# A first query projection without the token factor, a value projection woven into the recurrence's inverse, level masks on VectorE, and later output loads

## The chip, the core and the metric

The kernel runs on one core of one Trainium2 chip. The metric is the device time of one execution in microseconds (us); less is better. The engines are TensorE (PE; PEld are its weight loads), VectorE (DVE), ScalarE (ACT), GpSimd (POOL) and SyncE (SP), which issues most DMAs.

## The reference, cut to what matters

Three blocks run one after the other on 256 tokens of 1024 features, all in float32: a hybrid layer with three attentions and 16 experts, two attention layers, and two layers of feed-forward, gating (SGU) and an RWKV7 mixer. The change touches the first lines of the first block and the RWKV7 mixer of the third.

```python
def rmsnorm(x, g):
    y = x * lax.rsqrt(jnp.mean(x * x, axis=-1, keepdims=True) + EPS)
    return y * g
...
h = rmsnorm(x, attn_norm_g)
proj = h @ w_in                      # its first 1024 columns are da_q
...
# rwkv7_mixer; 16 heads of 64
xx = shifted(x) - x
r, k, v = (x + xx * mu[i]) @ w_rkv[i]
w = -softplus(-(w0 + tanh(xw @ w1) @ w2)) - 0.5
a = sigmoid(a0 + (xa @ a1) @ a2)
g = sigmoid(xg @ g1) @ g2
kk = k * k_k / norm(k * k_k);  k = k * (1 + (a - 1) * k_a)
# per token, with decay = exp(-exp(w)), a_t = -kk, b_t = kk * a:
state = state * decay + (state @ a_t) b_t^T + v k^T;  y = state @ r
y = groupnorm(y) * gn_g + gn_b
out = ((y + sum(r * k * r_k) * v) * g) @ w_o
```

## The kernel before

**Products in three terms.** Weights and activations of a dense product are split into a rounded high half and the rest ("hi" and "lo", type float32r). `t_three` (lines 582 to 584) makes each product from three matmuls: hi x hi, hi x lo, lo x hi. ACT makes the weights' high half (`a_hi`, line 544), DVE the low half (`v_lo`, line 555), each in two halves of a load of 1 MB, 128x1024 elements each. A load sits in a staging slot (four slots: units 32, 34, 36, 38 of on-chip memory, names `U_(u, n)`); its halves go to a "pair" of buffers. A slot is loaded again once both halves are made, a pair is written again once TensorE has used it (`pair_free`). `plan` writes the order of all loads; `sync` issues them in that order on SP, so that a load that waits holds back those behind it. `a_upto`, `a_ahead` and `v_upto`, `v_ahead` convert loads in order up to a number.

**The order of the work** on each engine is written by hand, with semaphores between engines; each engine runs its own list in order. PSUM has eight banks, handed out in turn by `Ring` (`FB`: 0 to 3, `KB`: 0 to 7); who takes a bank waits for the one who read it last.

**The start.** `t_mix`, `a_mix`, `v_mix` begin with the norm of x: ACT squares (line 886), TensorE sums them over features with a matrix of ones (line 877), ACT takes the root (904), DVE the reciprocal (`v_rstd`, 909: RSTD, one factor for each token), then eight times x times gain times RSTD (916, DVE), the high half (899, ACT) and the low half (922, DVE). TensorE runs eight filler matmuls (`t_idle`, 627) and then the four chunks of "daq", 48 matmuls of 256 columns each, whose results ACT evacuates (835). "dak" follows.

**The RWKV7 mixer.** `t_rwkv`, `a_rwkv`, `v_rwkv`, `g_rwkv`. TensorE makes k, the small products of w and a, and r, then z3 and z4 (line 2698, the gate's first product), the value projection "rwkv.v" (`t_proj_tm`, four chunks, each in two halves of 24 matmuls), and the gate's second product (2709, 2710). Meanwhile ACT makes the sigmoids of z3, z4 and then the three exponentials of the summed decay ("grow", 2955; "decay_before", 2959; "decay", 2962), and DVE the decayed b, a, k and r (3128, 3133, 3138, 3145) and the values without their mean (3152 to 3158).

The recurrence is done in chunks of 64 tokens: for each chunk and head a triangular 64x64 system is inverted. `t_cells` (2631) makes the 64 cells of one kind, 64x64 matmuls in float32, which the trace shows as 128 rows. First N, its transpose NT, the a rows by token (2726) and A2T. The inverse T doubles in five levels: X = (NT times the level's mask) T; T's transpose G by `to_g` (2740), and T = T + G X. ACT copies X and G (2984, 2993), DVE adds (3193). The masks of level 1 are DVE's (3180), those of levels 2 to 5 GpSimd's (3286). In each level TensorE has other work as well, `fill`: b and k by token (955), RBT, RKT with the bonus rows (2673), Z with the bonus (2763); DVE masks or copies these (3168, 3199). Behind the inverse come the changes of the chunks (2790), W1, W2, MT and QT (2807), the outputs (2823, at whose end stands the mark "chunks"), the passing of the state (2845, 2836), the group norm and the output projection "rwkv.o", whose four loads are all issued early.

## Time and profile before

| | |
|---|---|
| time, median of 3 runs | 2775.74 us (2774.43 to 2778.12) |
| the profiled execution: time, span | 2778.7 us, 2776.7 us |
| TensorE busy | 2339.0 us, 84% |
| VectorE, ScalarE, GpSimd busy | 1227.0, 931.3, 61.2 us |
| DMA | 695.46 MB, mean 250 GB/s |
| start to the first three-term matmul | 17.97 us |
| RWKV7 mixer and its surroundings | 2315 to 2580 us |
| from the first cells (N) to the first matmul behind the inverse | 2430.16 to 2509.16 us |

Times in the trace are from the start of the span; the run's time is 2.0 us longer than the span. In a timeline a line gives start, duration, engine and line of the kernel, operation, output and inputs with shapes, the number of instructions merged (x), and in brackets the idle time of that engine before it and what ended it; "issue" there means that nothing the profile shows was waited for. The PEclk of a stretch is the granted clock of TensorE, 1.00 being 2.4 GHz.

### The profile page before, as it was taken

To read this page: it belongs to the slowest core of one execution; us is meant where nothing else is said; L and a number is where in the kernel's file an instruction comes from. 1 tells how busy PE (TensorE), PEld (TensorE's weight loads), DVE (VectorE), ACT (ScalarE), POOL (GpSimd) and SP (SyncE) were. 2 spreads that over 40 slices of the span, in tenths; PEclk is the share of its full clock that TensorE was granted. 3 is DMA by queue.
4 is the path that set the end of the run, shared out by engine and by line. 5 is a ranking of instruction groups with operands and counts; after the bars stand their busy time and mean duration, and the time that the engine had idled before them with its cause. 6 is when DMAs were issued, how large, how long until landed. Compare 5 with 4: busy or idle time off the path is not lost.

```text
span 2776.7 us, 37696 instructions
## 1 busy us (share of the span) xinstructions
PE 2339.0 (84%) x16482; PEld 1668.4 (60%) x16482; DVE 1227.0 (44%) x1751; ACT 931.3 (34%) x1524; POOL 61.2 (2%) x36
## 2 busy tenths in 40 slices
PE   8999998656565565656889999999999999977998
PEld 8897785111111121111479888798887888866787
DVE  5667562000010000000387765576656548744654
ACT  5556541000000000000355654444454444632442
POOL 0000010000000000000000000000000000041000
PEclk9999999877878888887899999999999999999999
DMA  7543459999999999999734365575545553412552
GB/s 237 167 159 114 144 206 405 428 428 428 428 428 428 428 428 427 428 427 428 285 104 140 122 212 182 175 249 182 197 168 202 191 197 108 155 34 78 192 187 91
DMA packets 248645, 695.46 MB, mean 250 GB/s; under 512 B 11648, under 2 KB 191104, under 8 KB 222112
## 3 DMA queue, kind: packets, MB, share of 16 engines
q1 hardware_dynamic: 246176, 679.16, 64.3%
q0 software_dynamic: 2016, 13.67, 1.3%
q8 instruction: 130, 2.13, 0.3%
q14 instruction: 35, 0.29, 0.0%
q10 hardware_dynamic: 288, 0.22, 0.0%
HBM read 691.96 MB, written 1.05 MB: 250 GB/s over the span
## 4 chain that ended last, share of the span: by engine, by line
PE 58%; DMA 29%; DVE 8%; ACT 3%; issue 1%; SPq 1%; POOL 0%; ACTq 0%; DVEq 0%
PE ps L582 16%; PE ps L584 15%; PE ps L583 15%; DMA af<-in_w_exp_up 13%; DMA af<-in_w_exp_gate 9%; DMA af<-in_w_exp_down 6%; PE ps L1661 2%; DVE ar L555 1%; PE ps L2631 1%; SPq L513 1%; PE ps L877 1%; PE ps L1691 1%; ACT af L1057 1%; PE ps L2226 1%; DVE af L1096 1%
## 5 line engine op out<-in xcount | busy, mean ns | idle before, releaser
L582 PE MATMUL ps<-ar 128*128 128x512 f32 (+2 forms) x2648 | 925.1, 349 | 17.6 <-DVE ar L3276 2.9
L584 PE MATMUL ps<-ar 128*128 128x512 f32 (+2 forms) x2648 | 907.2, 343 | 0.0
L583 PE MATMUL ps<-ar 128*128 128x512 f32 (+2 forms) x2648 | 907.1, 343 | 0.0
L555 DVE TENSOR_TENSOR ar<-af,ar 128x1024 fp32r<-128x1024 f32 x516 | 604.2, 1221 | 288.3 <-ACT ar L544 288.2
L544 ACT ACTIVATE ar<-af 128x1024 fp32r<-128x1024 f32 x516 | 510.4, 1047 | 158.8 <-PE ps L584 142.5
L582 PEld LDWEIGHTS ps<-ar 128*128 128x128 f32 x2648 | 502.2, 190 | 93.3 <-issue 12.0
L584 PEld LDWEIGHTS ps<-ar 128*128 128x128 f32 x2648 | 502.2, 190 | 59.1
L583 PEld LDWEIGHTS ps<-ar 128*128 128x128 f32 x2648 | 502.9, 190 | 56.1 <-issue 0.5
L1661 PE MATMUL ps<-af 128*32 128x512 f32 x2048 | 329.6, 777 | 226.0 <-DMA af<-in_w_exp_up 120.0
L1661 PEld LDWEIGHTS ps<-af 128*32 128x32 f32 x2048 | 64.1, 127 | 476.1 <-DMA af<-in_w_exp_up 193.9
L1691 PE MATMUL ps<-af 128*32 128x512 f32 x1024 | 164.6, 769 | 99.9 <-DMA af<-in_w_exp_down 87.5
L1830 DVE TENSOR_TENSOR af<-af,ps 128x512 f32<-128x512 f32 x16 | 11.0, 688 | 538.0 <-ACT af L1737 538.0
L1737 ACT ACTIVATE af<-ps 128x512 f32<-128x512 f32 x16 | 9.6, 597 | 592.1 <-PE ps L1661 592.1
L1548 DVE TENSOR_TENSOR af<-ps,af 128x512 f32<-128x512 f32 x76 | 48.6, 685 | 296.1 <-PE ps L1703 273.5
L1691 PEld LDWEIGHTS ps<-af 128*32 128x32 f32 x1024 | 34.1, 126 | 212.5 <-DMA af<-in_w_exp_down 143.7
L1744 ACT ACTIVATE af<-ps 128x512 f32<-128x512 f32 x16 | 9.6, 597 | 270.2 <-PE ps L1691 270.2
L2286 DVE TENSOR_TENSOR af<-af,ps 128x256 f32<-128x256 f32 x66 | 27.8, 421 | 125.0 <-ACT af L2257 124.9
L2257 ACT ACTIVATE af<-ps 128x256 f32<-128x256 f32 x66 | 25.3, 384 | 135.7 <-PE ps L584 135.7
L1057 ACT ACTIVATE af<-af,sm 128x256 f32<-128x256 f32 (+1 forms) x136 | 64.0, 474 | 17.0 <-DVE sm L1143 10.0
L2631 PE MATMUL ps<-af 64*64 64x64 f32 x2304 | 43.3, 225 | 21.3 <-issue 19.0
L2631 PEld LDWEIGHTS ps<-af 64*64 64x64 f32 x2304 | 39.7, 137 | 23.9 <-issue 20.6
L2248 ACT ACTIVATE ar<-ps 128x512 fp32r<-128x512 f32 x44 | 26.3, 599 | 81.6 <-PE ps L2226 81.6
(313 smaller groups left out, 1633.5 us busy)
## 6 DMA issues: line engine op xcount, KB each, us to landing
af<-in_w_exp_gate SPq DMA_DIRECT2D x64, 2048.0 KB, 41.2
af<-in_w_exp_up SPq DMA_DIRECT2D x64, 2048.0 KB, 40.6
af<-in_w_exp_down SPq DMA_DIRECT2D x63, 2048.0 KB, 41.5
af<-in_ffn_w_in SPq DMA_DIRECT2D x88, 1024.0 KB, 5.8
af<-in_ffn_w_out SPq DMA_DIRECT2D x44, 1024.0 KB, 5.1
af<-in_w_in SPq DMA_DIRECT2D x34, 1024.0 KB, 5.3
af<-in_sgu_w_in SPq DMA_DIRECT2D x16, 1024.0 KB, 7.0
af<-in_w_out SPq DMA_DIRECT2D x12, 1024.0 KB, 5.3
```

The source lines that it names most:

```text
L513: e.dma_start(view(base), src).then_inc(*(self.row_in[r] if q == self.tail else self.landed[load.slot]).one())
L544: e.activation(self.WH[load.pair][:, c], self.base(i)[:, c], ACT.Copy).then_inc(*self.act.inc(("hi", i, h)))
L555: e.tensor_tensor(self.WL[load.pair][:, c], self.base(i)[:, c], f_(self.WH[load.pair][:, c]), ALU.subtract).then_inc(*self.dve.inc(("lo", ...
L582: e.matmul(o, lh, rh, start=start, stop=False, skip_group_check=True)
L583: e.matmul(o, lh, rl, start=False, stop=False, skip_group_check=True)
L584: return e.matmul(o, ll, rh, start=False, stop=stop, skip_group_check=True)
L1057: e.activation(d, d, ACT.Exp, bias=st[:, g:g + 1], accum_out=st[:, 4 + g:5 + g]).then_inc(*self.act.inc((name, "e", i, g)))
L1548: e.tensor_tensor(d, it(self.bank((name, c))), d, ALU.add).then_inc(*self.dve.inc(("out", name, c)))
L1661: t = e.matmul(ps[32 * j:32 * j + 32, bb, :], XE[:, k, c:c + 32], k_(self.base(q), 2)[:, r, 512 * j:512 * j + 512], start=k == 0, stop=k == 7)
L1691: t = e.matmul(ps[o:o + 32, b, :], self.AT_[x % 2][:, r * P + 32 * j:r * P + 32 * j + 32], k_(self.base(q), 4)[:, r, 512 * c:512 * c + 512 ...
L2286: e.tensor_tensor(G, G, up, ALU.mult).then_inc(*done)
L2631: t = e.matmul(self.ps[64 * r:64 * r + 64, banks[n], 64 * c:64 * c + 64], left(tt, h, i, cp), right(tt, h, i, cp), start=True, stop=True)
```

## The change

- The first query projection takes x times gain (new pair `xg`) in place of the normed x. DVE evacuates it and multiplies by RSTD and 0.125 (`q_out`). The normed x and its halves are made between the chunks, for "dak" and all behind it. The filler matmuls are gone, the root comes behind four gained copies.
- The value projection becomes eight steps (`next(v_halves)`), one before N, then behind X and behind T of the levels; the gate's second product comes in two parts, behind T of level 4 and of level 5. It has PSUM bank 7 to itself, `KB` has banks 0 to 6. Its weights all go through pair 0, in slots 2, 0, 1, 0; T and X of the inverse move to units 36 and 38, which were slots 2 and 3.
- In ACT's order the exponentials come ahead of the sigmoids of z3 and z4; value conversions, RKT, Z, the product r times k, the centred values and the decayed r move to other places of the inverse.
- The masks of levels 2 to 5 are made by DVE, two instructions a level, and GpSimd's four go.
- The loads of rwkv.o use slots 0 to 3; from the third on, SP waits for "chunks".

```diff
@@ -423,11 +423,14 @@
+        slots[:], count[0] = (2, 0, 1, 0, 1, 0, 1, 2, 3), 0
+        over_pairs(0)
...
+        slots[:], count[0] = range(4), 0
@@ -470,7 +473,7 @@
-            return [[self.pe.val(("ps", "Gt", 5, 1, 1))], [self.pe.val(("ps", "W2", 1, 1))], [self.pe.val("chunks"), self.pool.val("vb0")],
+            return [[self.pe.val(("used", before, h))], [self.pe.val(("ps", "W2", 1, 1))], [self.pe.val("chunks"), self.pool.val("vb0")],
@@ -507,6 +510,9 @@
...
+            if q == self.at["rwkv.o"] + 2:
+                for w in S.new(self.pe.val("chunks")):
                     e.wait_ge(*w)
@@ -1205,9 +1212,7 @@
-        self.t_idle(e, 7, 8)
-        daq = self.t_proj(e, "daq", 4, H, self.halves("n1"), DB, self.by_act("daq"))
-        run(daq)
+        run(self.t_proj(e, "daq", 4, self.xg, self.halves("xg"), DB, self.by_dve("daq")))
@@ -1298,16 +1303,22 @@
+        gained = lambda j: self.a_gained_hi(e, "xg", self.x, self.xg[0], lambda f: self.V("attn_norm_g", f), j, [])
+        gained(0)
...
+        gained(1)
+        self.a_hi(e, 0, 1)
+        gained(2)
+        gained(3)
...
-        self.a_hi(e, 0, 1)
...
-        self.a_normed(e, "n1", self.B(8), self.XP)
-        daq, dak = self.a_proj(e, "daq", 4, self.a_copy(F(self.daq), 0.125)), self.a_proj(e, "dak", 4, self.a_copy(F(self.dak)))
+        daq, dak = self.a_proj(e, "daq", 4), self.a_proj(e, "dak", 4, self.a_copy(F(self.dak)))
...
+            if step in (2, 4, 6):
+                self.a_normed(e, "n1", self.B(8), self.XP, {2: (0, 1, 2), 4: (3, 4, 5), 6: (6, 7)}[step])
@@ -1408,10 +1421,30 @@
-        self.v_upto(e, 0)
+        def gained_lo(j):
+            for f in (2 * j, 2 * j + 1):
+                for w in self.Vw.new(self.act.val(("xg", "h", f))):
+                    e.wait_ge(*w)
+                e.scalar_tensor_tensor(out=self.xg[1][:, f, :], in0=F(self.x)[:, f, :], scalar=self.V("attn_norm_g", f), in1=f_(self.xg[0][:, f, :]),
+                                       op0=ALU.mult, op1=ALU.subtract).then_inc(*dve.inc(("xg", "l", f)))
+        gained_lo(0)
+        self.v_lo(e, 0, 0)
+        gained_lo(1)
+        self.v_lo(e, 0, 1)
+        self.v_next = 1
+        gained_lo(2)
+        gained_lo(3)
...
-        run(self.v_normed(e, "n1", self.x, self.B(8), lambda f: ("attn_norm_g", f), self.XP))
-        daq, dak = self.v_proj(e, "daq", 4), self.v_proj(e, "dak", 4)
+        n1 = self.v_normed(e, "n1", self.x, self.B(8), lambda f: ("attn_norm_g", f), self.XP)
+
+        def q_out(e, name, c):
+            for w in self.Vw.new(self.pe.val(("ps", name, c)), dve.val(("n1", "rstd"))):
+                e.wait_ge(*w)
+            e.scalar_tensor_tensor(out=F(self.daq)[:, 2 * c:2 * c + 2, :], in0=it(self.bank((name, c))), scalar=0.125,
+                                   in1=self.RSTD.unsqueeze(1).broadcast_to((P, 2, T)), op0=ALU.mult, op1=ALU.mult).then_inc(*dve.inc(("out", name, c)))
+            for step in range(4 if c < 2 else 2 if c == 2 else 0):
+                next(n1, None)
+        daq, dak = self.v_proj(e, "daq", 4, q_out), self.v_proj(e, "dak", 4)
@@ -2573,7 +2606,7 @@
-        self.T_, self.X_, self.G4, self.NM, self.NT = U_(0, 2), U_(2, 2), U_(4, 2), (U_(14, 2), U_(6, 2)), self.cst[:, NFIRST:NFIRST + BIG]
+        self.T_, self.X_, self.G4, self.NM, self.NT = U_(36, 2), U_(38, 2), U_(4, 2), (U_(14, 2), U_(6, 2)), self.cst[:, NFIRST:NFIRST + BIG]
@@ -2633,7 +2666,7 @@
-        FB, KB = self.FB, Ring(*range(8))
+        FB, KB = self.FB, Ring(*range(7))
@@ -2697,10 +2730,11 @@
-        run(self.t_proj_tm(e, "rwkv.v", 1024, both(self.XV, F), self.halves("x2"), FB, self.by_act("rwkv.v")))
-        pe.mark("v_done")
+        v_halves = self.t_proj_tm(e, "rwkv.v", 1024, both(self.XV, F), self.halves("x2"), Ring(7), self.by_act("rwkv.v"))
+        next(v_halves)
...
-        for tt in range(2):
+
+        def gate(tt):
@@ -2748,10 +2782,11 @@
             elif lev == 3:
+                by_head("bonus_rows", self.selr, self.rkk, (dve, "bonus_rows"), [dve.val("rkk")], KB)
+            elif lev == 5:
...
-                by_head("bonus_rows", self.selr, self.rkk, (dve, "bonus_rows"), [dve.val("rkk")])
+                cells_z()
             elif lev == 4:
-                cells_z()
@@ -2770,12 +2805,21 @@
         for lev in range(1, 6):
...
-                         lambda tt: [dve.val(("NM1", tt)) if lev == 1 else pool.val(("NM", lev)), dve.val(("T", lev - 1, tt))])
+                         lambda tt: [dve.val(("NM", lev, tt)), dve.val(("T", lev - 1, tt))])
...
+            if lev < 5:
+                next(v_halves)
...
+            if lev < 4:
+                next(v_halves)
+            elif lev == 4:
+                run(v_halves)
+                gate(0)
+            else:
+                gate(1)
@@ -2960,17 +2999,18 @@
+        for n, m in (("z3", P), ("z4", 32)):
+            for w in self.Aw.new(pe.val(("ps", n))):
+                e.wait_ge(*w)
+            e.activation({"z3": self.z3, "z4": self.z4}[n], self.bank(n)[0:m, 0:T], ACT.Sigmoid).then_inc(*act.inc(n))
...
-        self.a_upto(e, v0 + 2)
-        v_out(0)
-        self.a_upto(e, v0 + 3)
-        for c in range(1, 4):
-            v_out(c)
-        for tt in range(2):
+        self.a_next = o0
+
+        def gate(tt):
@@ -3002,13 +3042,26 @@
         for lev in range(1, 6):
+            if lev == 1:
+                self.a_hi(e, v0 + 1, 0)
+            elif lev < 4:
+                self.a_hi(e, v0 + lev, 0)
+            elif lev == 5:
+                gate(0)
...
+            if lev < 4:
+                self.a_hi(e, v0 + lev, 1)
+            if lev < 5:
+                v_out(lev - 1)
...
+                for w in self.Aw.new(dve.val("r_decayed")):
+                    e.wait_ge(*w)
...
-            elif lev == 4:
+            elif lev == 5:
...
+        gate(1)
@@ -3132,30 +3184,21 @@
-        self.v_upto(e, v0 + 2)
...
-        self.v_upto(e, v0 + 3)
...
+
+        def centred():
+            v3 = self.VV.rearrange("p (a v) -> p a v", v=64)
+            for w in self.Vw.new(act.val(("out", "rwkv.v", 3))):
+                e.wait_ge(*w)
+            e.tensor_reduce(self.vmean, v3, AX.X, ALU.add).then_inc(*dve.inc("v_sums"))
...
@@ -3167,22 +3210,32 @@
-        masked("N", "ml0", self.T_, "N", [pe.val("v_done")])
+        masked("N", "ml0", self.T_, "N", [pe.val("r_done"), pe.val(("ps", "z4")), act.val(("hi", v0, 1)), dve.val(("lo", v0, 1))])
...
-        for tt in range(2):
-            t = lambda m: m[:, tt * 1024:tt * 1024 + 1024].rearrange("p (a s) -> p a s", s=64)
-            for w in self.Vw.new(act.val(("NT", tt, 1))):
-                e.wait_ge(*w)
-            e.tensor_tensor(t(self.NM[1]), t(self.NT), bc("mu1", 16), ALU.mult).then_inc(*dve.inc(("NM1", tt)))
+
+        def level_mask(lev, ready=()):
+            for tt in range(2):
+                t = lambda m: m[:, tt * 1024:tt * 1024 + 1024].rearrange("p (a s) -> p a s", s=64)
+                for w in self.Vw.new(act.val(("NT", tt, 1)), *ready):
+                    e.wait_ge(*w)
+                e.tensor_tensor(t(self.NM[lev % 2]), t(self.NT), bc("mu%d" % lev, 16), ALU.mult).then_inc(*dve.inc(("NM", lev, tt)))
+        level_mask(1)
...
         masked("A2T", "upp", self.A2T, "A2T", [])
+        for w in self.Vw.new(act.val("decay")):
+            e.wait_ge(*w)
+        e.tensor_copy(self.PC, self.S1.rearrange("p (f c t) -> p f c t", f=8, c=4)[:, :, :, 63]).then_inc(*dve.inc("decayed"))
+        for w in self.Vw.new(act.val("decay"), act.val(("out", "rwkv.r", 3))):
+            e.wait_ge(*w)
+        e.tensor_tensor(R_, R_, self.S1, ALU.mult).then_inc(*dve.inc("r_decayed"))
+        self.v_lo(e, v0 + 1, 0)
@@ -3199,22 +3252,41 @@
         for lev in range(1, 6):
             if lev == 1:
+                for w in self.Vw.new(dve.val("r_decayed")):
+                    e.wait_ge(*w)
...
+                self.v_lo(e, v0 + 1, 1)
+                level_mask(2, [pe.val("kk_free")])
...
+                self.v_lo(e, v0 + 2, 0)
...
+                level_mask(3, [pe.val(("X done", 1))])
...
-                masked("RKT", "uppi", self.RKT, "RKT", [])
+                self.v_lo(e, v0 + 3, 0)
...
+                level_mask(4, [pe.val(("X done", 2))])
...
-                cells("Z", self.Z, (1,), [pe.val(("ps", "RKT", 1, 1)), dve.val("rkk")])
+                level_mask(5, [pe.val(("X done", 3))])
...
+            else:
+                masked("RKT", "uppi", self.RKT, "RKT", [])
+                cells("Z", self.Z, (1,), [pe.val(("ps", "RKT", 1, 1)), dve.val("rkk")])
...
+            if 1 < lev < 4:
+                self.v_lo(e, v0 + lev, 1)
+            if lev == 1:
+                for w in self.Vw.new(dve.val("r_decayed"), dve.val("k_grown"), pe.val(("ps", "zw")), dve.val(("x2", "l", 7))):
+                    e.wait_ge(*w)
+                e.tensor_tensor(self.rkk, R_, K_, ALU.mult).then_inc(*dve.inc("rkk"))
+            elif lev == 4:
+                centred()
+        self.v_next = o0
@@ -3280,19 +3352,10 @@
-        def level(lev, ready):
-            for w in self.Gw.new(act.val(("NT", 1, 1)), *ready):
-                e.wait_ge(*w)
-            e.tensor_tensor(m3(self.NM[lev % 2]), m3(self.NT), self.C("mu%d" % lev).unsqueeze(1).broadcast_to((P, 32, 64)),
-                            ALU.mult).then_inc(*pool.inc(("NM", lev)))
-        level(2, [pe.val("kk_free")])
-        level(3, [pe.val(("X done", 1))])
...
-        level(4, [pe.val(("X done", 2))])
-        level(5, [pe.val(("X done", 3))])
```

## Rows read from the trace of the kernel before

**Rows 1.** The page: TensorE's total, busy tenths in 40 slices, instruction queue.
```profile
PE 2339.0 (84%) x16482; PEld 1668.4 (60%) x16482; DVE 1227.0 (44%) x1751; ACT 931.3 (34%) x1524; POOL 61.2 (2%) x36
...
PE   8999998656565565656889999999999999977998
...
q8 instruction: 130, 2.13, 0.3%
```

**Rows 2.** Stretches: length, busy of each engine, granted clock, DMA share, GB/s.
```profile
430.00:1356.00 926.00, 575.90 (x3594) 162.40 (x3593) 84.09 (x158) 28.96 (x49) 0.00 (x0) 0.81 1.00 426
...
2315.00:2550.00 235.00, 199.81 (x4197) 178.54 (x4196) 143.48 (x227) 107.51 (x183) 41.20 (x13) 0.98 0.26 85
```

**Rows 3.** Timeline of the start, all engines.
```profile
6.94 2.19 ACT L886 ACTIVATE af<-af 128x512 f32<-128x512 f32 x4 [3.92 <-DMA cst<-in_consts]
...
7.71 6.16 PE L877 MATMUL ps<-af,cst 128*128 128x256 f32 x16 [7.71 <-ACT af L886]
...
14.42 1.75 DVE L909 RECIPROCAL sm<-sm 128x256 f32<-128x256 f32 x1
...
17.97 0.35 PE L582 MATMUL ps<-ar 128*128 128x256 f32 x1 [0.64 <-ACT ar L899]
...
25.10 0.60 ACT L835 ACTIVATE af<-ps 128x512 f32<-128x512 f32 x1 [3.51 <-PE ps L584]
...
30.86 0.60 ACT L835 ACTIVATE af<-ps 128x512 f32<-128x512 f32 x1 [3.27 <-PE ps L584]
```

**Rows 4.** Timelines of DVE, ACT and PE ahead of the first cells.
```profile
2403.69 2.49 DVE L3133 SCALAR_TENSOR_TENSOR af<-af 128x512 f32<-128x512 f32 x4
...
2399.53 1.91 ACT L2955 ACTIVATE af<-af 128x2048 f32<-128x2048 f32 x1
...
2397.74 0.39 PE L582 MATMUL ps<-ar 128*128 128x256 f32 x1
...
2421.73 1.12 PE L2709 MATMUL ps<-af 128*128 128x512 f32 x2 [0.69 <-ACT af L2967]
...
2430.16 3.14 PE L2631 MATMUL ps<-af 64*64 64x64 f32 x199
```

**Rows 5.** Timeline of PE in the inverse's end.
```profile
2504.89 0.49 PE L2631 MATMUL ps<-af 64*64 64x64 f32 x16 [1.70 <-issue]
...
2509.16 2.08 PE L2790 MATMUL ps<-af 64*64 64x64 f32 x96 [1.27 <-ACT af L2993]
2512.49 2.24 PE L2631 MATMUL ps<-af 64*64 64x64 f32 x128 [1.25 <-issue]
2516.51 2.18 PE L2631 MATMUL ps<-af 64*64 64x64 f32 x127 [1.78 <-issue]
2520.38 0.21 PE L2631 MATMUL ps<-af 64*64 64x64 f32 x1 [1.69 <-issue]
```

**Rows 6.** PE's waits from 2420 to 2545 us: total, times, longest.
```profile
PE ps L2631 <- issue: 19.0, 14, 3.7
```

**Rows 7.** DMA from 2508.5 to 2512.5 us, in 40 slices of 0.1 us.
```profile
GB/s 0 0 0 0 0 0 0 0 0 0 0 0 0 0 0 0 164 0 0 0 0 0 0 0 0 0 0 0 0 0 0 0 0 0 0 0 0 0 0 0
```

**Rows 8.** Stretches: the cells NT and A2T, then level 2.
```profile
2437.00:2444.00 7.00, 6.99 (x165) 6.53 (x168) 2.94 (x5) 2.21 (x4) 0.00 (x0) 0.57 0.02 5
2456.20:2467.70 11.50, 8.62 (x386) 7.90 (x386) 4.85 (x8) 4.22 (x8) 2.96 (x3) 1.00 0.09 33
```

**Rows 9.** Groups by line from 2430 to 2545 us.
```profile
L3193 DVE TENSOR_TENSOR af<-af,ps 128x512 f32<-128x512 f32 x20 | 12.6, 683 | 14.7 <-PE ps L2631 14.7
...
L2740 PE MATMUL ps<-cst,af 128*128 128x128 f32 x96 | 12.5, 278 | 2.6 <-issue 2.2 <-DVE af L3193 0.4
...
L555 DVE TENSOR_TENSOR ar<-af,ar 128x1024 fp32r<-128x1024 f32 x4 | 4.7, 1220 | 3.3 <-ACT ar L544 3.3
...
L544 ACT ACTIVATE ar<-af 128x1024 fp32r<-128x1024 f32 x4 | 4.0, 1053 | 1.8 <-PE ps L2631 1.8
```

**Rows 10.** The loads of rwkv.o, from issue to landing.
```profile
DMA to landing us min/median/max: 5.2/6.3/10.6
```

## What I predict, and how it is worked out

> **What bounds the kernel now.** I read the page first. TensorE is busy 84% of the span; in the 40 slices it is nearly full outside the 8th to the 19th [rows 1]. The table of stretches names the bound by stage: from 430 to 1356 us the DMAs (share 1.00, 426 GB/s, the experts' weights), before and behind it TensorE, and the 235 us of the recurrence have only 199.8 us of TensorE work [rows 2]. So two places can give time back: the start, before TensorE gets its first projection, and the holes in the recurrence. A gain at the start is kept, since up to 430 us the order is TensorE's, and the experts' loads open by marks of that order and then run at a fixed rate.
>
> The start, in order of time [rows 3]: the ones-matmul for the token sums ends at 13.9 us. Then come the root (ACT), its reciprocal (DVE, 1.75 us), and the products and halves of each eighth, while TensorE runs filler. Its first projection matmul is at 17.97, and the first groups of three wait for the eighths as DVE and ACT make them. The chunks end one every 5.76 us, the first near 25.0, so the projection ends near 42.3.
>
> The recurrence [rows 4]: TensorE ends the gate's first product at 2397.7, runs the value projection until 2420.8 (192 matmuls at 0.12), the gate's second product from 2421.7 to 2430.2 (8.4 us), and only then the first cells, "N". What N needs was ready earlier: ACT's exponentials came after a conversion and two sigmoids, and the last decayed keys were done on DVE at 2406.2.
>
> From N to the first matmul behind the inverse, at 2509.16, are 79.0 us [rows 4, 5]. The list of waits puts 19.0 us of the idle time ahead of the cells up to 2545 to "issue" [rows 6]. I place these holes by counting: between two of them lie 127 or 128 matmul rows, each with its weight load, as from 2512.49 (x128) to 2516.51 (x127) to 2520.38 [rows 5]. The kernel has 2 x 16482 TensorE instructions and 130 packets on the instruction queue, 254 to a packet [rows 1], so a hole is the wait for the next packet. The block of instructions from 2504.89 (16 rows of cells, twice 8 transposes, 96 rows) lasted 6.35 us and still ended in a hole of 1.25. So the next block isn't asked for on entry: one is seen at about 2510.1, and work resumed at 2512.49 [rows 5, 7]. All this fits one reading: the request goes out some 32 matmul rows into a block and the next block can run 3.35 us later. Of dense rows the remaining 96 take 1.65 us, so a dense block costs a hole of 1.7 and a pitch of 3.9. The pitches 4.02 and 3.87 agree [rows 5].
>
> **The change, part by part.** *First projection.* It works on x times gain, without the root. ACT: squares until 9.13, two gained copies (0.42 each as the same form has), a weight half (1.06) and so on; the fourth pair of copies ends at 14.0. DVE: low halves of eighths 0 and 1 by 10.9, weight half by 12.3, eighths 2 and 3 by 13.2, second weight half 14.4, eighths 4 to 7 by 16.1. TensorE wants the first at 13.9 and the second half (24 matmuls later) at 16.8: no wait. The root then comes 1.7 us later than before (table, root, reciprocal until 17.9), and DVE's low halves of chunk 1 at 19.1 and 20.2, wanted at 19.7 and 22.5. DVE now evacuates each chunk (128x512 from PSUM, nearest row 0.68 [rows 9], bounds 0.6 and 0.8) and makes two to four normed eighths behind it, about 3.8 us for a 5.76 us chunk; low halves of chunks 2 and 3 come at 24.5 and 30.6, wanted at 25.4 and 31.2. The margin is half a microsecond, so up to 1.2 us can be lost. The normed halves are all there at 34.2, wanted by the next projection at 37.0. End of the projection: 13.9 + 4 x 5.76 = 36.9 instead of 42.3. Gain **5.3 us**, 4.1 if the margins fail. The filler that goes cost nothing that anyone waited for; the projection now follows the sums without a gap.
>
> *N earlier.* Without conversion and sigmoids between, ACT starts the exponentials at 2392.6 and ends the second, at 1.9 each [rows 4], at 2396.4; DVE's keys still wait for the gate's matmuls, which read the same place, until 2397.7, and take 2.5. TensorE fills this with the first of eight halves of the value projection (24 matmuls, 2.88). N starts at 2400.65 instead of 2430.16: **29.5 us** earlier.
>
> *What the inverse gets.* Seven halves (20.2) and the gate's second product (8.4): 28.6 us of TensorE work. If nothing of it is hidden the two nearly cancel (gain 0.9). The holes are what can be filled, but one only goes if slow work lies behind the 32nd row of its block. I walked the new order in instructions. Blocks begin at 78 + 256k from the first value matmul (before, one began 57 rows before the end of the cells "NT"; 16 filler rows are gone). Of the 19 blocks up to the end of the inverse, ten stay dense at their end and keep 1.6 to 1.75 us each (in N/NT, A2T, X1, RBT, T2, X3, T3, X4, Z, T5), the others are covered by a value half, transposes or the gate but for 0.35. Sum of holes 17.3. TensorE's work there: 16 sets of cells x 2.2, transposes 1.9 + 3.5 + 11.4 (96 of them have 12.5 with their modelled ends [rows 9]), bonus 1.3, and 28.6, in all 81.8. Waits for DVE in level 1: 0.9 (next part). The last wait for the G copies stays at 1.3, as before [rows 5]. 2400.65 + 81.8 + 17.3 + 0.9 + 1.3 = 2501.95 against 2509.16: gain **7.2 us**. In it is 1.8 us for a clock that was granted at 0.57 (1.2 GHz) from 2437 to 2444, after the hole of 3.7 us [rows 8]; that hole had the output weights' load beside it until 2435, and those loads now come later.
>
> The Trainium skill ("Runtime: NRT & Kernel Launch", Instruction fetch mechanics) has instructions come in blocks of 16 KiB, 256 instructions, which the trace agrees with (254). It also says that crossing a boundary is mostly hidden; here it is not, at 1.2 to 1.8 us each. What its rule would make of the time stands with the second rival.
>
> *Level masks.* GpSimd's four become eight of DVE at 1.22 (a low half has the same form [rows 9]), 9.8 us in all. In level 1 DVE has copies, low half, mask and additions in a row from 2422.2 to 2431.6, where TensorE wants the first at 2430.4: 0.9 lost. In the later levels DVE has 10 us of work for 16 to 18 us. If its cover is gone, a mask pair ahead of the additions costs 2.4 a level, 9.8 in all.
>
> *Value weights through one pair and three slots.* A half's conversion (1.05 on ACT, 1.22 on DVE [rows 9]) waits for the half before last; between are a level's cells, at least 5 us. Loads: value chunk 3 after DVE's low half of chunk 1 (2427), landed 2433, converted 2449; gate weights issued near 2449, wanted 2476. At nothing, with 2.3 per exposed half.
>
> *Output loads.* SP's last two now wait for "chunks" (2537.7 before, about 2530.5 now); behind them in SP's queue stand the ffn loads (first at 2512.5 before). Loads took 5.2 to 10.6 us, median 6.3 [rows 10], so 2536.7 and 2539; ACT's conversion of the first stands at 2546.26 - 7.2 = 2539.1. Hidden by 2.4; at 10.6 us it costs about 2. The ffn weights are next converted 30 us later.
>
> **Sum.** 5.3 + 7.2 = 12.5. The profiled execution took 2778.7, its span 2776.7; it gives 2766.2. From the median, 2775.7: 2763.2, my prediction **2763**. The runs shown spread over 3.7 us, so 0.2% (5.6 us) is about what a measurement can tell from no change.
>
> **Rivals.** *Half gain*: DVE's chain or the blocks fall badly, and the inverse hides nothing: 5.3 + 0.9, less up to 3 of DVE waits: 2769.5 to 2772.5. For it: ten of 19 blocks already stay dense. Against: the 3.7 us hole and the cold stretch go whichever way the blocks fall. *All filled*: holes and waits alike give way to the added work, by a deeper fetch after slow work or since the holes are latency of ACT and DVE: at most 79.0 less 53.2 of work less the 1.3 = 24.5, some 20 if other waits stay; with 0.9 and 5.3 in all 26 to 31: 2745 to 2750. That is where the skill's "mostly hidden" leads. For it: the holes end near ACT's and DVE's copies; against: the 6.35 us block with its hole. A partial case, fetch eased by the slow halves' run-ahead, gives 2753 to 2758. *Slower*: the single pair. Each of six later halves can queue on ACT behind X and G copies (2.07 each) and on DVE behind additions (2.48), 2.3 + 4.1 + 2.5 = 8.9, less the 5 us between halves 3.9: 23.4 in all, and the kernel 2787. It decides from 2.1 a half, where the whole gain is gone. Against: ACT was busy 4 to 5 us of each 12 us level [rows 8]. *No first part*: TensorE stalls on weights or DVE at chunks 1 to 3, gain 1: 2767.5.
>
> **How the numbers follow.** Forecast (both parts, 8 to 18 us gained) 0.60; all or nearly all filled 0.15; half gain 0.13; no first part 0.07; slower 0.05. Half gain lies on both sides of 2770.2, no first part below it. Faster by over 0.2%: 0.60 + 0.15 + 0.07 + 0.04 = 0.86; within 0.2%: 0.09; slower: 0.05. Leaving out the slower case and the full filling gives 2751 to 2771; the forecast's own range is 2758 to 2768.
>
> **What the profile after would show.** First three-term matmul near 13.9 us, its pace 0.12 at once, chunk 3's end near 37; a break shows as a wait for DVE's low halves. In the recurrence: N near 2395 (2400.65 less the 5.3), about ten holes of 1.7 put to "issue", still 127 or 128 rows apart, none of 3.7, granted clock 1.00 throughout. If the holes are fewer than five the second rival holds; if TensorE waits for the low halves or level masks, the slower ones. The prediction goes wrong most easily by the phase of the blocks, which I know to some 20 instructions, each flip being 1.7 us, and by the DVE margin at the start.

## The result

The changed kernel takes **2751.6 us** (median of four runs, 2749.44 to 2752.37), the kernel before, in runs between them on the same chip, 2776.43 (2774.43 to 2778.12). The ratio is 0.9909, 95% interval 0.9898 to 0.992: 25 us faster, within 22 to 28. I had predicted 2763, 12.5 faster, with a range down to 2751. The sign and the range held; the gain was twice the forecast.

The page of the profile after; its answer to [rows 1]:

```profile
PE 2318.2 (84%) x16466; PEld 1657.8 (60%) x16466; DVE 1244.8 (45%) x1771; ACT 931.3 (34%) x1528; POOL 44.0 (2%) x32
...
PE   8999998655656556655799999999999999998998
...
q8 instruction: 129, 2.11, 0.3%
```

The stretches that answer to [rows 2]:

```profile
430.00:1356.00 926.00, 565.80 (x3593) 157.61 (x3592) 83.85 (x152) 28.86 (x49) 0.00 (x0) 0.83 1.01 425
2309.00:2524.00 215.00, 195.13 (x4186) 176.02 (x4186) 155.32 (x234) 106.17 (x182) 23.87 (x9) 0.98 0.25 80
```

The experts are bound by DMA as before. The recurrence does nearly the same TensorE work (195.1 us for 199.8) in 215 us instead of 235.

The start, timelines of ACT and PE, which answer to [rows 3]:

```profile
7.22 2.19 ACT L892 ACTIVATE af<-af 128x512 f32<-128x512 f32 x4 [4.20 <-DMA cst<-in_consts]
...
7.99 5.47 PE L883 MATMUL ps<-af,cst 128*128 128x256 f32 x16 [7.99 <-ACT af L892]
...
13.11 0.47 PE L588 MATMUL ps<-ar 128*128 128x256 f32 x1
```

The first three-term matmul follows the sums without a gap, at 13.11 instead of 17.97. The projection's four chunks end at 36.8 us instead of 42.3, so 5.5 earlier. Where the mixer begins (VectorE's difference of neighbouring tokens) the kernel is 6.1 us ahead: 2320.59 for 2326.64.

The timeline of PE in the recurrence, with every hole of over 0.4 us; to be read against [rows 4, 5]:

```profile
2394.75 2.42 PE L2664 MATMUL ps<-af 64*64 64x64 f32 x146
2398.22 1.85 PE L2664 MATMUL ps<-af 64*64 64x64 f32 x110 [1.04 <-issue]
...
2405.48 2.20 PE L2664 MATMUL ps<-af 64*64 64x64 f32 x128 [1.42 <-DVE af L3211]
2409.11 0.39 PE L588 MATMUL ps<-ar 128*128 128x256 f32 x1 [1.44 <-issue]
...
2430.46 3.88 PE L2664 MATMUL ps<-af 64*64 64x64 f32 x243
2435.77 0.47 PE L2664 MATMUL ps<-af 64*64 64x64 f32 x13 [1.43 <-issue]
...
2450.28 0.48 PE L2664 MATMUL ps<-af 64*64 64x64 f32 x15 [1.03 <-issue]
...
2474.46 0.75 PE L2664 MATMUL ps<-af 64*64 64x64 f32 x34 [0.42 <-issue]
2478.20 2.08 PE L2664 MATMUL ps<-af 64*64 64x64 f32 x117 [1.54 <-issue]
2487.76 2.08 PE L2834 MATMUL ps<-af 64*64 64x64 f32 x96 [1.37 <-ACT af L3033]
2491.43 2.27 PE L2664 MATMUL ps<-af 64*64 64x64 f32 x128 [1.28 <-issue]
2495.18 1.02 PE L2664 MATMUL ps<-af 64*64 64x64 f32 x46 [1.47 <-issue]
```

From N (L2664, first row) to the first matmul behind the inverse (L2834) are 93.0 us; it was 79.0, and 28.6 us of work were added. So 14.6 of the 28.6 are hidden. Holes there are seven, 8.3 us in all; none is over 1.6. Before, those over 0.3 us made 19.1, so shorter holes are 10.8 of the 14.6; the half clock behind the hole of 3.7 [rows 8], which is gone, is part of the rest. The list of PE's waits from 2384 to 2520 us, which answers to [rows 6] (19.0, 14 times, longest 3.7):

```profile
PE ps L2664 <- issue: 8.2, 7, 1.5
PE ps L2851 <- DVE af L3252: 1.5, 1, 1.5
PE ps L588 <- issue: 1.4, 1, 1.4
```

Where the 26.1 us between the two spans (2776.7 and 2750.6) came from: 6.1 up to the mixer; 15.3 from there to the first matmul behind the inverse (N comes 29.4 earlier, the inverse is 14.0 longer); 3.0 behind it, to the group norm (2509.16 to 2546.67 before, 2487.76 to 2522.23 after); and 1.6 in the output projection, whose first chunk took 14.7 us before (2552.17 to 2566.86) and 13.1 after (2527.74 to 2540.83). The five us in which it begins differ in the granted clock; the kernel before first:

```profile
2552.00:2557.00 5.00, 4.83 (x14) 3.88 (x15) 5.00 (x8) 1.85 (x3) 0.00 (x0) 0.66 0.83 254
```

The kernel after:

```profile
2527.50:2532.50 5.00, 4.76 (x21) 3.99 (x22) 5.00 (x8) 1.92 (x3) 0.00 (x0) 1.00 1.05 351
```

This split is of one execution of each kernel. Six kernels below have the same TensorE order as the changed one up to N, and there N began anywhere from 2392.5 to 2397.2. Five executions with the same TensorE order up to the end of the inverse, the changed kernel's two among them, took 92.1 to 94.0 us from N to the first matmul behind the inverse. From there to the output projection the changed kernel took 40.0 us and 42.1 when it was run again, the kernel before 43.0. So the 15.3 stands well clear of this scatter, and the 3.0 and the 1.6 don't.

### The profile page after: what moved, and what is told of

It reads as the page before. It is cut to its first block, busy times and chain, and to the rows that moved or that the text cites. A ratio compares the mean times of both kernels' runs of the same rounds, so it can differ in the third digit from the quotient of the medians.

```text
span 2750.6 us, 37681 instructions
## 1 busy us (share of the span) xinstructions
PE 2318.2 (84%) x16466; PEld 1657.8 (60%) x16466; DVE 1244.8 (45%) x1771; ACT 931.3 (34%) x1528; POOL 44.0 (2%) x32
## 4 chain that ended last, share of the span: by engine, by line
PE 58%; DMA 30%; DVE 8%; ACT 3%; issue 1%; POOL 0%; ACTq 0%; DVEq 0%; SPq 0%
PE ps L588 16%; PE ps L590 16%; PE ps L589 16%; DMA af<-in_w_exp_gate 12%; DMA af<-in_w_exp_up 10%; DMA af<-in_w_exp_down 7%; PE ps L1694 2%; DVE ar L561 2%; PE ps L2664 1%; PE ps L1724 1%; PE ps L883 1%; PE ps L2259 1%; PE ps L1171 1%; ACT af L1063 1%; PE ps L1015 0%
## 5 line engine op out<-in xcount | busy, mean ns | idle before, releaser
L1063 ACT ACTIVATE af<-af,sm 128x256 f32<-128x256 f32 (+1 forms) x136 | 64.0, 474 | 17.7 <-DVE sm L1149 10.8
L2664 PE MATMUL ps<-af 64*64 64x64 f32 x2304 | 41.7, 224 | 10.9 <-issue 8.2
L1051 ACT ACTIVATE af<-ps 128x384 f32<-128x384 f32 (+1 forms) x60 | 29.7, 537 | 58.5 <-PE ps L1015 58.4
```

Source lines behind the costliest of these rows:

```text
L1051: e.activation(self.PT()[:, m, 0:at[1].stop], self.ps[:, 4 + m, 0:at[1].stop], ACT.Copy).then_inc(*self.act.inc((name, "p", i, m)))
L1063: e.activation(d, d, ACT.Exp, bias=st[:, g:g + 1], accum_out=st[:, 4 + g:5 + g]).then_inc(*self.act.inc((name, "e", i, g)))
L2664: t = e.matmul(self.ps[64 * r:64 * r + 64, banks[n], 64 * c:64 * c + 64], left(tt, h, i, cp), right(tt, h, i, cp), start=True, stop=True)
```

## The experiments

Each ran on one chip with the kernel before between its runs; the ratio is to that. The changed kernel, run again in the second group, is the measure of noise.

### Each part alone

`first_alone` is the kernel before with the first projection's edits only: in `t_mix`, `a_mix` and `v_mix` of the diff above the gained halves, the late root and `q_out`.

```diff
-        self.t_idle(e, 7, 8)
-        daq = self.t_proj(e, "daq", 4, H, self.halves("n1"), DB, self.by_act("daq"))
-        run(daq)
+        run(self.t_proj(e, "daq", 4, self.xg, self.halves("xg"), DB, self.by_dve("daq")))
```

> The kernel before with the first projection's part of the change alone. If the two parts add, it is 6.1 us faster than before (the projection ends at 36.2 instead of 42.3 us and nothing behind it gives that back): 2770.3. Rival: part of the gain is lost at the experts' loads, or half the gain of the changed kernel came from here: less than 4 or more than 9 us.

Measured: 2765.92 us (2761.84 to 2770.02, 7 runs), ratio 0.9969 (0.9958 to 0.998), 8.7 us faster (5.5 to 11.7). I had expected 6.1, which lies within that interval. In its trace the projection behind the RWKV7 mixer is 8.7 us early, but only 5.5 of it were there at the gate's second product (2416.19 for 2421.73): the rest came inside the recurrence, whose order it does not touch. It has 16 matmul rows fewer ahead of it, so the blocks of instructions begin elsewhere. That suggested that the holes depend on the phase; one trace can't show it.

`recurrence_alone` is all the rest of the change without the first projection.

```diff
+            if q == self.at["rwkv.o"] + 2:
+                for w in S.new(self.pe.val("chunks")):
...
+            if lev < 5:
+                next(v_halves)
```

> The kernel before with every part of the change but the first projection. If the parts add, it keeps 24.8 less 6 to 8.6: 16 to 19 us faster than before, about 2757. Rival: the parts meet in the phase of the instruction blocks (the first part takes 32 instructions out), then the holes in the inverse stand 16 rows later and the gain differs by a hole or two, 1.5 to 3 us.

Measured: 2764.01 us (2760.02 to 2766.76, 5 runs), ratio 0.9948 (0.9934 to 0.9962), 14.4 faster, where I had expected 16 to 19. The parts add to 23.1 of 24.8. From N to the first matmul behind the inverse this execution took 100.3 us, not 93.0, and holes explain little of it: those put to issue there make 9.1 us (8.1 ahead of cells, 1.0 ahead of a transpose), 0.8 more than the 8.3. The clock did: from 2489.1 us on TensorE was granted half, through the gate's second product and the transposes, 13.0 us up to the end of the inverse. Timeline of PE; two matmul rows of 512 columns take 2.07 us, 1.12 in [rows 4]:

```profile
2488.77 0.45 PE L2637 MATMUL ps<-af 64*64 64x64 f32 x5 [1.75 <-issue]
2489.14 2.07 PE L2716 MATMUL ps<-af 128*128 128x512 f32 x2
...
2497.15 3.67 PE L2747 MATMUL ps<-cst,af 128*128 128x128 f32 x16
```

### What the holes hang on: the phase of the blocks

Ten, and then 32, matmuls that nobody reads, in expert 8, where DMA sets the pace; they shift every later block by 20 and by 64 rows.

```diff
+            for n in range(10 if x == 8 else 0):
...
+                j = n % 4
+                e.matmul(ps[32 * j:32 * j + 32, ba, :], XE[:, 0, c:c + 32], k_(self.base(q), 2)[:, 0, 512 * j:512 * j + 512],
+                         start=True, stop=True)
```

> The changed kernel with 10 needless matmuls in expert 8, where the weights' loads set the pace: 20 rows of PE, 40 instructions, so that every block of 256 instructions (128 rows of PE) behind them begins 20 rows earlier in the program. Theory A: a block costs TensorE a hole of 3.65 us less the time of its own matmuls and waits, if that is above zero. By the rows of the changed kernel's trace from N's first cell to the first matmul behind the inverse, cut into blocks where the trace has its holes, this gives holes of 1.5, 0.5 to 1.4, 1.65, 1.35, 1.4, 1.4 (measured 1.04, 1.44, 1.43, 1.03, 0.42, 1.54) and about 8.9 in sum; cut 20 rows earlier it gives ten holes and about 13, among them one in each of N (behind its cell 126), T1, RBT, X3 (1.4) and T4 that are not there now. So the stretch from N to the first matmul behind the inverse takes about 97 us instead of 93.0, and the kernel about 2755 to 2756, 4 above the changed one. Theory B: the holes belong to places of the program (a value half ahead, a semaphore, a load beside): they stay behind N's 146th cell and T2's 243rd, and the time within 1 us of the changed kernel.

> The same with 32 needless matmuls in expert 8: 64 rows of PE, half a block. Theory A: N's hole comes behind its cell 82 instead of 146 (or lies in the next block, behind 210), T2's behind cell 179 instead of 243; the sum of holes from N to the first matmul behind the inverse is by the same reckoning about 7.5 (fewest of all cuts), so this stretch takes 91.5 to 92.5 us and the kernel is 0 to 2 us faster than the changed one: 2750 to 2752. Theory B: holes where they are, same time.

Measured: 20 rows, 2757.62 us (2755.73 to 2762.46, 5 runs), ratio 0.9933 (0.9921 to 0.9946); 64 rows, 2750.77 (2748.73 to 2751.93, 4 runs), 0.9906 (0.989 to 0.9921). N's hole came where theory A has it in both, T2's in the one of 64 rows; the time of 64 rows is as foretold, that of 20 rows 1.6 us above. Timeline of PE from N, 20 rows:

```profile
2395.02 2.09 PE L2670 MATMUL ps<-af 64*64 64x64 f32 x126
2399.00 2.09 PE L2670 MATMUL ps<-af 64*64 64x64 f32 x128 [1.89 <-issue]
2402.75 0.32 PE L2670 MATMUL ps<-af 64*64 64x64 f32 x2 [1.65 <-issue]
...
2407.67 2.19 PE L2670 MATMUL ps<-af 64*64 64x64 f32 x127 [0.93 <-issue]
```

And 64 rows:

```profile
2394.70 3.36 PE L2670 MATMUL ps<-af 64*64 64x64 f32 x210
2399.10 0.92 PE L2670 MATMUL ps<-af 64*64 64x64 f32 x46 [1.04 <-issue]
```

N's first hole moves from behind row 146 to behind row 126 and row 210 (82 + 128). N to the first matmul behind the inverse takes 98.1 and 91.6 us, for 93.0 (foretold 97 and 91.5 to 92.5). So the same text of the recurrence costs 6.5 us more or less by where code far ahead of it has put the blocks. Theory B is out. Counted from the start of the program, the holes don't move. The kernel of 20 rows has holes behind 12158, 12286, 12540, 13175 and 14447 of TensorE's matmul rows, the changed one behind the first, third and fourth of these, that of 64 rows behind all but the first. Where one is missing, the block ahead of that place holds slow work. How large each is was foretold less well. Of the places named for 20 rows (N, T1, RBT, X3, T4) only N had a hole; the other new ones came at the end of NT, in a value half and in T5.

### Where the value halves stand

```diff
-            if lev < 5:
+            if lev == 1:
                 next(v_halves)
             to_g(lev - 1)
             fill(lev)
+            if 1 < lev < 5:
+                next(v_halves)
```

> The changed kernel, with the value halves of levels 2 to 4 that stood behind X moved between the level's other cells and T. The work is the same. If the holes are waits for instruction blocks, the one between RBT and T of level 2 (1.43 us) and the one in T of level 3 (1.03) go, since slow matmuls now stand between dense cells: 1 to 2.5 us faster. Rival: the holes are latencies of ACT's copies of X and G; these now lie behind the half, and T would gain as well, but the additions and X would not: then the waits of T on ACT change and those put to issue don't.

Measured: 2756.85 us (2753.27 to 2757.53, 5 runs), ratio 0.9925 (0.9912 to 0.9938). Its median is 4 above that of the changed kernel run again beside it (next run), but the intervals overlap. I had expected a gain of 1 to 2.5.

The changed kernel run again, as the measure of noise:

> The changed kernel once more, beside the others on the same chip: 2749 to 2753, 22 to 25 us faster than before.

Measured: 2753.01 us (2750.26 to 2753.41, 4 runs), ratio 0.9913 (0.9899 to 0.9927).

In the trace of `half_before_t` one hole had doubled. Timeline of PE, then the DMAs from 2433 to 2439 us in slices of 0.15:

```profile
2433.00 2.02 PE L2664 MATMUL ps<-af 64*64 64x64 f32 x115
2437.90 0.47 PE L2664 MATMUL ps<-af 64*64 64x64 f32 x13 [2.88 <-issue]
```

```profile
GB/s 137 218 109 246 300 437 355 410 410 437 437 437 355 219 137 82 137 0 0 0 0 0 0 0 0 0 0 0 0 0 0 0 0 0 0 0 0 0 0 0
```

That is GpSimd's load of the group norm's two rows (0.5 MB each); the packet of instructions is inside it. In the changed kernel the packet (the 82 at 2433.4) had gone ahead of the same loads; from 2430 to 2438 us in slices of 0.2:

```profile
GB/s 0 0 0 0 0 0 0 0 0 0 0 0 0 0 0 0 0 82 0 0 143 205 307 389 266 246 205 225 205 205 348 348 410 410 369 328 307 123 143 61
```

So the next kernel moves these loads behind X of level 3 as well.

```diff
-        for w in self.Gw.new(pe.val("bv_free")):
+        for w in self.Gw.new(pe.val("bv_free"), pe.val(("X done", 3))):
```

> The changed kernel with the value halves of levels 2 to 4 moved to between the fill and T, as in the run before of that name, and GpSimd's two loads of the norm's rows (0.5 MB each, which there moved at 2431 to 2436 us) behind X of level 3 as well. Theory A: in that run the block behind T2's first cells had to be fetched beside these loads, and so its hole was 2.88 instead of 1.43, and the clock was granted low for the 4 us behind it; without them the hole is 1.2 to 1.5, the clock 1.00, and the stretch from N to the first matmul behind the inverse 95.4 - 1.5 - 1.5 = 92.5 us: the kernel takes 2752 to 2754 (2756.85 then). Theory B: the hole is 2.88 because the block behind 115 cells is late by itself: the stretch stays at 95 and the time at 2756 to 2757.

Measured: 2752.81 us (2749.78 to 2753.3, 4 runs), ratio 0.9912 (0.9898 to 0.9925). The 2.88 is gone altogether (I had left 1.2 to 1.5), the clock from 2430 to 2450 is 1.00, and N to behind the inverse takes 91.5 us instead of 95.4. So the load had made the hole. Whether the halves' new place gains anything isn't shown: 91.5 is 0.6 below the lowest of the five executions with the old place, and `three_moves`, which has the new one, took 92.6. The whole kernel isn't measurably faster than the changed one, and its interval overlaps that of `half_before_t`.

### The output weights' loads

`before_o_late` is the kernel before with its last two output loads held until level 1's X.

```diff
+            if q == self.at["rwkv.o"] + 2:
+                for w in S.new(self.pe.val(("X done", 1))):
+                    e.wait_ge(*w)
```

> The kernel before; SP alone waits for the end of X of level 1 ahead of the third output load. In the kernel before, the third and fourth load ran beside the cells N and NT, where the hole was 3.7 us and the granted clock fell to 0.57 behind it. If loads beside the cells delay the next block of instructions, that hole is 1.3 to 1.8 us here, the clock stays, and the kernel is 2 to 4 us faster than before. Rival: the 3.7 us has another cause (a bank, a latency of ACT): no change.

Measured: 2773.86 us (2772.11 to 2779.53, 11 runs), ratio 0.9992 (0.9983 to 1.0001): 2 us, not to be told from nothing. The trace shows the mechanism all the same. The hole of 3.72 that stood in NT is 0.98, with the clock at 1.00 from 2433 to 2440, and from N to the first matmul behind the inverse are 75.3 us, not 79.0; but a new one of 3.15 has come behind the inverse, beside a load of the ffn weights that came at 2508. Timeline of PE:

```profile
2433.15 1.05 PE L2634 MATMUL ps<-af 64*64 64x64 f32 x57 [0.98 <-issue]
...
2513.35 3.82 PE L2634 MATMUL ps<-af 64*64 64x64 f32 x128 [3.15 <-issue]
```

`loads_at_g5` is the changed kernel with those loads released by G of level 5, some 30 us sooner.

```diff
-                for w in S.new(self.pe.val("chunks")):
+                for w in S.new(self.pe.val(("ps", "Gt", 5, 1, 1))):
```

> The changed kernel, but SP waits for the last transposes of the inverse, not for the mark chunks, before the third output load. ACT's wait of 0.8 us for that load is gone. If weight loads beside the dense cells delay the instruction blocks, holes between 2486 and 2516 us grow by 1 to 4 us in all, and the kernel is 0 to 3 us slower. Rival: they don't touch each other, and the kernel is the same or 1 us faster.

Measured: 2756.75 us (2753.01 to 2758.36, 5 runs), ratio 0.9939 (0.9927 to 0.9952), above the changed kernel's 0.9898 to 0.992, though the interval touches that of its second run (0.9899 to 0.9927): slower, by 4 to 8 us. ACT's wait of 0.8 us for the last load is gone, but the hole at 2491 went from 1.28 to 4.02, and the cells behind it took 3.80 us, not 2.27. Timeline of PE:

```profile
2491.88 3.80 PE L2664 MATMUL ps<-af 64*64 64x64 f32 x128 [4.02 <-issue]
```

In the trace that is 2.7 + 1.5 - 0.8 = 3.4 us, which the late loads of the change save. I had put them at nothing. The 1.5 is the clock, granted at half from 2489.9 to 2496.7.

### Level masks, and GpSimd's last products

`pool_masks` is the changed kernel with the masks of levels 2 to 5 back on GpSimd.

```diff
-                level_mask(2, [pe.val("kk_free")])
...
+        level(2, [pe.val("kk_free")])
```

> The changed kernel with the masks of levels 2 to 5 made by GpSimd again. If moving them to DVE is worth nothing, the same time within 2 us. Rival: GpSimd's four masks of 4.5 us run beside DVE's low halves in the levels (both read two operands from on-chip memory) and stretch them, so that TensorE waits: 3 us or more slower.

Measured: 2752.01 us (2750.73 to 2754.88, 5 runs), ratio 0.9923 (0.9911 to 0.9936). No difference to the changed kernel (0.9909 and 0.9913) can be seen: 0.9 us was the price I gave, too small for these runs.

`gate_behind` makes GpSimd's last two products wait for VectorE's low halves of the first output chunk. In the changed kernel's timeline of DVE and of POOL these stood side by side:

```profile
2488.66 7.70 DVE L561 TENSOR_TENSOR ar<-af,ar 128x1024 fp32r<-128x1024 f32 x2 [6.79 <-ACT ar L550]
...
2485.27 4.54 POOL L3372 TENSOR_TENSOR af<-af 128x2048 f32<-128x2048 f32 x1 [3.45 <-ACT af L3017]
2489.89 5.39 POOL L3375 TENSOR_TENSOR af<-af 128x2048 f32<-128x2048 f32 x1
```

```diff
-        for w in self.Gw.new(pool.val("vb"), act.val(("g", 1, 1))):
+        for w in self.Gw.new(pool.val("vb"), act.val(("g", 1, 1)), dve.val(("lo", self.at["rwkv.o"], 1))):
```

> The changed kernel, with GpSimd's last two products (4.5 and 5.4 us) held until DVE has the low halves of the first output weights. In the changed kernel these two low halves took 7.70 us beside GpSimd, where they otherwise take 2.35. If GpSimd is what stretches them, they take 2.4 us here, DVE's copies of W1 come 4 us sooner, and the kernel is 1 to 3 us faster. Rival: the stretch comes from something else (the output loads, the clock), or TensorE's wait is the next block of instructions anyway: no change.

Measured: 2750.06 us (2748.51 to 2751.57, 5 runs), ratio 0.9915 (0.9902 to 0.9929). The two subtractions fall from 7.70 to 2.36 us, and TensorE's last scan matmul ends 29.9 us behind the start of the first matmul behind the inverse, not 33.2. Not all of these 3.2 are the subtractions: in the changed kernel's execution TensorE was granted half the clock over 10 us of that stretch, and here the full one. The changed kernel first:

```profile
2496.50:2506.70 10.20, 8.12 (x262) 7.99 (x265) 4.21 (x7) 2.83 (x4) 0.00 (x0) 0.50 0.02 5
```

```profile
2496.50:2506.70 10.20, 6.88 (x337) 6.50 (x329) 6.15 (x10) 2.70 (x4) 4.08 (x1) 1.00 0.01 3
```

The second run of the changed kernel had the full clock there too. In it the scan's products W1 to QT (L2851) begin 12.1 us behind the inverse, here 10.6: some 1.5 us, by one execution of each, can be put to the subtractions. Timeline of DVE, then the ten us in which the output projection begins (2525.26):

```profile
2488.90 2.36 DVE L561 TENSOR_TENSOR ar<-af,ar 128x1024 fp32r<-128x1024 f32 x2 [6.80 <-ACT ar L550]
```

```profile
2519.00:2529.00 10.00, 7.83 (x32) 6.11 (x32) 9.56 (x12) 6.15 (x9) 0.00 (x0) 0.83 1.08 368
```

The clock fell in the output projection, from whose first chunk to the second went 14.7 us for 13.1, and behind it the kernels stand within 1 us of each other. The contention is shown; a gain in the kernel's time is not.

### Three moves together

Value halves, norm loads and GpSimd's products, each as in the diffs above, on the changed kernel.

> The changed kernel with the three moves tried so far together: value halves of levels 2 to 4 between fill and T, GpSimd's loads of the norm's rows behind X of level 3, and GpSimd's last two products behind VectorE's low halves for the output projection's first chunk. Theory A: the gains add where they lie on the chain. N to the first matmul behind the inverse takes 91.5 to 92.5 us (93.0 in the changed kernel), VectorE's two 128x1024 subtractions behind the inverse take 2.4 us instead of 7.7, and the scan's stretch is 3 us shorter; the output projection's first chunk is at a granted clock of 0.57 for 4 us, as in the run of that last move alone, and gives 1.6 back: 2751.6 - 1 - 3 + 1.6, so 2748 to 2750. Theory B: what is saved ahead of the output projection is given back whole by the clock, as in that run: 2750 to 2752.

Measured: 2750.07 us (2747.59 to 2751.68, 4 runs), ratio 0.991 (0.9894 to 0.9927). N to behind the inverse took 92.6 us and the subtractions 2.36, and the output projection's first chunk again 14.7. No measurable gain over the changed kernel: the median lies on the border of theory A (2748 to 2750) and B (2750 to 2752), and the run doesn't decide between them. 64 rows of idle code, these three moves, and the change as made all lie from 2750 to 2753.

## Why the prediction was right in sign and half in size

**First projection, 5.3 us.** Right. The first matmul came without a gap and behind its first sums TensorE waited for nothing in the first 60 us, so the margin of half a microsecond held. Measured in the trace: 5.5 at the projection's end, 6.1 where the mixer begins. The part alone gave 8.7 (5.5 to 11.7); in its trace the surplus lies in the recurrence, where it shifts the blocks by 16 rows.

**N earlier, 29.5 us.** Right: 29.4.

**The inverse, 7.2 us net.** This is the step that was mis-sized: it was 15.3, and the term is the **sum of holes**, "ten stay dense at their end and keep 1.6 to 1.75 us each ... 17.3". There were seven with 8.3 us, level 1's 0.9 of DVE waits and its block among them; the work there was 82.8 for 81.8. Those foreseen in RBT, X3 and X4 did not come, the others had 1.2 on average.

My reading was that the request for the next block goes out some 32 rows into a block, so that only slow work behind that row hides it. The holes after fit another better: a block can follow some 3.7 us after the one before it *starts*, so a hole is 3.7 less the block's own time, whichever part of it is slow. Cut every 127 or 128 rows at the places that the holes fix, the trace after gives by my rule 16.3 us of holes from N to T5, among them 2.0 in RBT, 1.2 in X3 and 1.0 in X4, where there are none. The other gives 11.4, with one of 0.7 in RBT that isn't there and 1.55 where 0.42 was measured; the trace has 8.3. So the other is nearer and has all the places, but is still 3 us too high. A dense block took 3.3 to 4.0 us from start to start (3.75 from 2399.00 to 2402.75 in the run of 20 rows). A block with a value half (2.9 us for 24 rows) takes 4.7 us, and in the changed kernel none had a hole.

The instruction packets in the traces say where the time goes. In all 14 traces, before and after among them, TensorE's first row behind a hole of over 0.35 us put to issue between 2385 and 2525 us ran 2.2 to 2.9 us after the start of a 16 KB packet on the instruction queue: 140 holes, short and long. In a dense block behind a hole the packet mostly starts 1.0 to 1.3 us after the block's first row. A wait for a semaphore can hold it back. The block of 6.35 us with a hole of 1.25 [rows 5], which had misled me, has 96 rows that waited for ACT until 2509.16, near its 32nd row, and the packet came just after [rows 7]; the changed kernel has the same sight, 96 rows behind a wait until 2487.76, a packet at 2488.78, a hole of 1.28. That a wait restarts the count is my explanation. Two blocks don't fit the rule of 3.7 even so: that of 20 rows from 2402.75 had 4.0 us of work, half of it in 16 transposes, and a hole of 0.93, and one with a value half in the kernel of 64 rows had 5.2 us of work and a hole of 0.62, beside GpSimd's loads. The runs with 20 and 64 rows came near the foretold sums of holes (about 13 and 7.5 us, measured 12.3 and 6.0), the first with most of its new holes elsewhere than foretold. They show that the phase of the blocks sets the holes; the size of each is known only roughly, and what sends the request stays open. The rival "a partial case, fetch eased by the slow halves' run-ahead", 2753 to 2758, is the one that came nearest.

By the Trainium skill ("Runtime: NRT & Kernel Launch", Instruction fetch mechanics) crossing a block is mostly hidden. That held for most blocks with slow work, and not for dense ones, at 1.0 to 1.5 us for most in the changed kernel.

**No hole of 3.7, clock 1.00.** Half right. The long hole went, and with it the clock of 0.57 behind it; but behind the inverse, from 2496.5 to 2506.7, the granted clock was at half, which I had not foreseen. The 1.6 us in the output projection came from a clock that stayed up there; in the second run of the changed kernel it stayed up there too (13.1 us for that chunk), and it did in `before_o_late`, so by these traces it is luck and no effect of the change.

**Behind the inverse, nothing.** Off by 3.0 in this pair of executions, by 0.9 with the changed kernel's second run (43.0, 40.0 and 42.1 us up to the output projection). The kernel before had holes of 1.25, 1.78 and 1.69 there [rows 5], which my sum left as they were; after they are 1.28, 1.47 and none, by phase again. GpSimd's work beside VectorE's costs about 1.5 more in this stretch (`gate_behind`).

**Level masks, single pair, output loads, nothing.** Masks: no difference seen. The pair: no wait for it in the trace. Loads: hidden but for 0.8 of ACT's wait, while what they no longer disturb is worth 3.4 net of that in the trace of `loads_at_g5`.

**Rivals.** "Half gain" and "slower" rested on waits for DVE or the pair, and none over 1.5 us came in the inverse. "All filled", 2745 to 2750, was nearly met by the kernel with 64 rows.

## What to carry to other kernels

Dense small matmuls (here 17 ns each) run out of instructions. Count 128 rows from one hole to the next, and put a slow piece of work into each block that has none. Expect the whole to shift by several us when code far ahead gains or loses a few instructions, and test a change at two or three phases before its gain is put down to its reason. Keep bulk loads out of the moment at which such a block is fetched. Before a gain of 2 to 3 us is banked, look at what the clock does next, and at how much the same stretch differs between two executions of one kernel.

## What the runs showed of the hardware

**A load beside a block's fetch can double the hole.** Seven holes of 2.33 to 4.02 us were seen in five kernels (before, `first_alone` three times, `before_o_late`, `half_before_t`, `loads_at_g5`), all among the cells and each beside a load where the packet was due; without one, holes were 0.3 to 1.8. Moving the load took 3.72 to 0.98 and 2.88 to nothing, and put 4.02 where 1.28 had been. What is late is the packet's start, 2.1 to 6.9 us after the block's first row; from there to the next block's first row it is 2.3 to 2.6 us as elsewhere. But a load isn't enough: fourteen holes with a load at 340 GB/s or more from the block's first row to its packet were 0.7 to 1.9. What decides stays open.

**The clock fell behind such holes, but not only there.** In or just behind each of those seven it went to half (0.57 [rows 8]; behind the 4.02, 128 cells in 3.80 us instead of 2.3), but in `recurrence_alone` also behind holes of 1.43 and 1.75. In the same program it differed between executions: the changed kernel had it low in the scan in one and, run again, just ahead of the output projection. What sets it stays open.

**VectorE beside GpSimd.** A subtraction 128x1024 with both inputs in on-chip memory took 3.85 us instead of 1.18 beside GpSimd's products, and GpSimd's product 5.39 instead of 4.54. The Trainium skill ("GPSIMD Engine Reference", 1. Specifications) says that the two share their interfaces to this memory, with contention when VectorE has two inputs there; the trace agrees, at a factor of 3.3 for VectorE.
